# Two transformer blocks on one core: norm factor applied to the products' results, stages of block two placed beside dense chunks

## The chip, the cores and the metric

One core of a Trainium2 chip runs the whole computation. The metric is device time in microseconds, the median of three runs. The engines are TensorE (PE: matmul, and PEld: its weight load), VectorE (DVE), ScalarE (ACT), GpSimd (POOL) and SyncE (SP), whose queue issues the DMAs.

## What is computed

x has 512 tokens of width 1024, float32. Block one:

```python
z = rms_norm(h, attn_norm) @ w_in
o = concat(nsa_mixer(...), gla_mixer(...))
h = h + o @ w_out
u = causal_dwconv(rms_norm(h, ffn_norm) @ w_up, conv_w, conv_b)
h = h + (silu(gate) * up) @ w_down
```

`nsa_mixer` is softmax attention with compressed, selected and window parts; `gla_mixer` is gated linear attention in chunks of 64. Block two puts 16 meta tokens in front, so that it has 528:

```python
proj = rmsnorm(h, gain) @ w_in
q, k = l2norm(silu(conv4(dq))), l2norm(silu(conv4(dk)));  v = silu(conv4(dv))
o_dn = rmsnorm(gated_delta_rule(q, k, v, g, beta)) * silu(dz)
o_sb = stick_breaking_attention(rmsnorm(sq), rmsnorm(sk), sv)
merged = sigmoid(gate_dn) * (o_dn @ w_branch_dn) + sigmoid(gate_sb) * (o_sb @ w_branch_sb)
h = h + merged @ w_out
h = h + (silu(gate) * up) @ w_ffn_out
```

Every `rms_norm` is x * rsqrt(mean(x^2) + eps) * gain: a factor per token and a gain per channel.

## The kernel before

**Layout and the stream of weights.** Activations lie with channels on partitions: `K.h` holds the residual as 8 tiles of 128 x 512. All dense weights come as one stream of 285 chunks of 128 x 1024 floats (512 KB). SP loads chunk n into one of two raw buffers (`load_chunk`, L251 to L256); ScalarE rounds it to the fast float format (`whi`, L269); VectorE writes the remainder (`wlo`, L276). Three such pairs are in use (HL = 3): when TensorE has used chunk s (`K.s_used`), ScalarE makes chunk s + 3 (`split_hi`, `split_lo`). A product is three matmuls, w_hi x_hi, w_hi x_lo and w_lo x_hi (`three`, L291 to L293), so the input x has a high and a low part too (`K.nx_hi`, `K.nx_lo`). A chunk is 8 k-tiles of one output tile of 128 channels: 24 matmuls for 512 tokens, 48 for 528 tokens in two halves of 264.

**Stages.** Each stage is a `Block`: all engines start it together, each runs its own list in order, and semaphores tie them; at the end all meet. `sems` clears the semaphores of a past stage on GpSimd. The order of the stages:

1. `start` (L493): loads x, constants, parameters; squares of x, sums over channels with matmuls (`norm_sums`, L445), root, reciprocal, factor spread over partitions with matmuls (`norm_spread`, L454), then `norm_scale` multiplies x by gain and factor (L484), ScalarE rounds (`norm_hi`, L467), VectorE subtracts (L479). The same for the meta tokens.
2. `project1`: 16 chunks with tokens on the output partitions (`product_rows512`, L413 to L415) and 8 chunks with channels there (`product_cols`).
3. `nsa_prepare`, `nsa_compressed`, `nsa_attend`, `gla`: the mixers of block one.
4. `out_ffn` (L574): the output product (8 chunks) added to `K.h`, after each tile its square and its sums on TensorE; then `norm_spread` and `norm_scale`; the up product (44 chunks, with the 3-tap convolution read from PSUM, L720 to L742); the down product (22 chunks), again with squares and sums per tile, and at the end the norm for block two.
5. Block two, `delta_gates`: one chunk for the gates' logits, small matmuls, and a chain of activations.
6. For each of two groups of four heads: `project_conv` twice (8 chunks each, 4-tap convolution and SiLU, L1481 to L1492), `norm_cols` (squares, sums with 16-column matmuls L1397, root, reciprocal L1422, spread with 16-row matmuls L1405, scaling L1429), `delta_rows` (transposes as matmuls L1612, scaled copies), `delta_rule` with 8 chunks of the gate `dz` placed among its small matmuls (`Side`, L1697; ScalarE copies the results, L1990), `delta_output` (row norm, SiLU, transposes L2106), then the branch product: 8 chunks for group 0, and 16 chunks in `merge_pairs` for group 1 (gate and branch in turn).
7. Attention: `project_plain` three times (8 chunks each), `transpose_units`, `norm_cols` over 16 heads, `stick_breaking`, `split_stage`, `merge_last` (16 chunks: 8 gates, 8 branch).
8. `out_ffn` for block two (no convolution, no next norm), with the store of the result.

In a `product_cols` stage two pairs of PSUM banks alternate, and ScalarE (or VectorE) frees them with a copy; `out_ffn` rotates over four banks. VectorE, ScalarE and TensorE queues are strictly in program order, so a step waits for every step that stands before it on its engine.

## Time and profile before

| | us |
|---|---|
| median of 3 runs | 2732.98 (2722.13 to 2749.69) |
| the profiled execution | 2740.02 |
| its span in the trace | 2737.9 |
| mean granted TensorE clock | 0.91 |

A group's row gives line, engine, operation, output<-input, shapes and count, then busy time and the mean of one, then the idle time of the engine before it and what ended it. A window's row gives start:end and length, then for each engine busy time and instruction count, then the granted TensorE clock (1.00 is 2.4 GHz, 0.50 is 1.2 GHz), the share of DMA engines busy, and GB/s. A timeline's row gives start and duration. One float32 matmul with float32 operands leaves two records in the trace (two passes).

### The profile page before, as it was taken

To read this page: it belongs to the slowest core of one execution; us is meant where nothing else is said; L and a number is where in the kernel's file an instruction comes from. 1 tells how busy PE (TensorE), PEld (TensorE's weight loads), DVE (VectorE), ACT (ScalarE), POOL (GpSimd) and SP (SyncE) were. 2 spreads that over 40 slices of the span, in tenths; PEclk is the share of its full clock that TensorE was granted. 3 is DMA by queue.
4 is the path that set the end of the run, shared out by engine and by line. 5 is a ranking of instruction groups with operands and counts; after the bars stand their busy time and mean duration, and the time that the engine had idled before them with its cause. 6 is when DMAs were issued, how large, how long until landed. Compare 5 with 4: busy or idle time off the path is not lost. (4 is left out here: it accounts for less than half of the span.)

```text
span 2737.9 us, 32980 instructions
## 1 busy us (share of the span) xinstructions
PE 2441.1 (89%) x13996; PEld 1887.7 (69%) x13996; DVE 1042.2 (38%) x1588; ACT 829.1 (30%) x1350; POOL 36.2 (1%) x68
## 2 busy tenths in 40 slices
PE   5976997799999968799698799699989989999999
PEld 4854555578888858666478666488966467788887
DVE  3234353445553235434525444432122124433322
ACT  2223234134442233222323222322233632322221
POOL 0000000000000000000000000000001200000000
PEclk9986598599999979789899899899997999999999
DMA  3231000022333212000022011032210022223322
GB/s 118 93 93 47 1 1 1 24 70 93 98 95 93 93 39 78 23 32 25 9 85 78 24 32 32 16 92 78 85 39 0 1 77 85 69 93 96 97 93 92
DMA packets 48354, 163.31 MB, mean 60 GB/s; under 512 B 5072, under 2 KB 9552, under 8 KB 48208
## 3 DMA queue, kind: packets, MB, share of 16 engines
q1 hardware_dynamic: 48208, 161.20, 18.6%
q8 instruction: 111, 1.82, 0.3%
q14 instruction: 35, 0.29, 0.0%
HBM read 158.04 MB, written 2.10 MB: 58 GB/s over the span
## 5 line engine op out<-in xcount | busy, mean ns | idle before, releaser
L291 PE MATMUL ps<-nx_hi,whi 128*128 128x512 f32 (+1 forms) x1936 | 680.0, 351 | 74.1 <-ACTq L361 24.1
L292 PE MATMUL ps<-nx_lo,whi 128*128 128x512 f32 (+1 forms) x1936 | 676.2, 349 | 0.0
L293 PE MATMUL ps<-nx_hi,wlo 128*128 128x512 f32 (+1 forms) x1936 | 675.0, 349 | 0.0
L276 DVE TENSOR_TENSOR wlo<-raw,whi 128x1024 fp32r<-128x1024 f32 x282 | 345.1, 1224 | 781.0 <-ACT whi L269 781.0
L269 ACT ACTIVATE whi<-raw 128x1024 fp32r<-128x1024 f32 x282 | 298.1, 1057 | 764.3 <-PE ps L293 693.1
L291 PEld LDWEIGHTS ps<-nx_hi,whi 128*128 128x128 f32 x1936 | 374.1, 193 | 128.9 <-issue 67.3
L292 PEld LDWEIGHTS ps<-nx_lo,whi 128*128 128x128 f32 x1936 | 375.4, 194 | 46.0
L293 PEld LDWEIGHTS ps<-nx_hi,wlo 128*128 128x128 f32 x1936 | 374.6, 193 | 46.0
L291 PE MATMUL ps<-act_hi,whi 128*128 128x512 f32 x352 | 139.6, 396 | 0.0
L292 PE MATMUL ps<-act_lo,whi 128*128 128x512 f32 x352 | 139.1, 395 | 0.0
L293 PE MATMUL ps<-act_hi,wlo 128*128 128x512 f32 x352 | 139.0, 395 | 0.0
L291 PE MATMUL ps<-o_hi,whi 128*128 128x512 f32 x192 | 77.0, 401 | 7.8 <-ACTq L361 7.8
L293 PEld LDWEIGHTS ps<-act_hi,wlo 128*128 128x128 f32 x352 | 66.0, 187 | 16.2
L292 PEld LDWEIGHTS ps<-act_lo,whi 128*128 128x128 f32 x352 | 66.0, 188 | 15.9
L291 PEld LDWEIGHTS ps<-act_hi,whi 128*128 128x128 f32 x352 | 66.0, 188 | 15.8
L292 PE MATMUL ps<-o_lo,whi 128*128 128x512 f32 x192 | 76.8, 400 | 0.0
L293 PE MATMUL ps<-o_hi,wlo 128*128 128x512 f32 x192 | 76.6, 399 | 0.0
L1154 ACT ACTIVATE probs<-ps,max 128x128 f32<-128x128 f32 (+3 forms) x64 | 33.8, 528 | 120.9 <-DVE max L1111 120.9
L1405 PE MATMUL ps<-rt,const_sb 16*128 16x264 f32 x128 | 57.4, 646 | 14.0 <-DVE rt L1423 14.0
L1062 PE MATMUL ps<-kT,qT 64*128 64x128 f32 (+3 forms) x128 | 62.6, 575 | 1.4 <-PEq L969 1.4
L1405 PEld LDWEIGHTS ps<-rt,const_sb 16*128 16x128 f32 x128 | 42.0, 331 | 28.8 <-DVE rt L1423 15.6
L1697 PE MATMUL ps<-nx_hi,whi 128*128 128x512 f32 x128 | 58.0, 453 | 2.8 <-PEq L1596 2.8
(428 smaller groups left out, 3019.6 us busy)
## 6 DMA issues: line engine op xcount, KB each, us to landing
raw<-stream_dram SPq DMA_DIRECT2D x285, 512.0 KB, 3.5
h_sb<-x_dram SPq DMA_DIRECT2D x4, 512.0 KB, 5.4
cmp_w<-cmp_w_k_dram SPq DMA_DIRECT2D x4, 512.0 KB, 4.5
cmp_w<-cmp_w_v_dram SPq DMA_DIRECT2D x4, 512.0 KB, 3.9
out_dram<-h_sb SPq DMA_DIRECT2D x8, 256.0 KB, 4.9
const_sb<-const_dram SPq DMA_DIRECT2D x1, 816.5 KB, 8.4
param_sb<-param_dram SPq DMA_DIRECT2D x1, 774.0 KB, 9.7
const<-const_dram SPq DMA_DIRECT2D x1, 616.0 KB, 4.0
```

Source lines behind the costliest of these rows:

```text
L269: act.activation(K.whi[:, n % HL], K.raw[:, n % RAW], ACT.Copy).then_inc(K.s_hi, 1)
L276: dve.tensor_tensor(K.wlo[:, n % HL], K.raw[:, n % RAW], K.whi[:, n % HL].bitcast(F32), ALU.subtract).then_inc(K.s_lo, 1)
L291: pe.matmul(out, whi, xhi, start=start, stop=False, skip_group_check=skip)
L292: pe.matmul(out, whi, xlo, start=False, stop=False, skip_group_check=skip)
L293: return pe.matmul(out, wlo, xhi, start=False, stop=stop, skip_group_check=skip)
L1062: pe.matmul(out, R.qT[b0:b0 + 64, h // 2, t * P:(t + 1) * P], R.kT[b0:b0 + 64, 2 * b + g, 0:ext], start=True, stop=False, skip_group_check ...
L1154: act.activation(pr[:, u % 2, b, 0:(t + 1) * P], K.ps[:, 2 * (u % 2) + b, 0:(t + 1) * P], ACT.Exp, bias=mx[:, u % 2, b:b + 1], accum_out=s ...
L1405: mm = pe.matmul(K.ps[:, 2 + 2 * (i % 3) + h, 0:HALF], cst(K, "ident", 16)[:, i:i + 1].broadcast_to([16, P]), rt[:, a:e], start=True, stop ...
L1697: mm = pe.matmul(K.ps[:, 6 + c % 2, :], w, x, start=j == 0, stop=j == SIDE_CHUNK - 1, skip_group_check=True)
```

## The change

**Norm factor on the result.** Products take x times gain, without the token factor. `residual_hi` and `residual_lo` make its parts from `K.h` directly; the squares are summed over the 8 tiles on VectorE (`residual_acc`), so that `norm_sums` needs 8 matmuls in all. The factor is spread once into `K.fac` (SBUF), and VectorE multiplies each product's result by it when it leaves PSUM.

```diff
+def residual_hi(K, act, z, d, gain, ready):
+    act.wait_ge(z["added"], ready)
+    act.activation(K.nx_hi[:, d, META:T2], K.h[:, d], ACT.Identity, scale=gain[:, d:d + 1]).then_inc(z["nx_hi"], 1)
...
+    act.activation(K.sq[:, d % 2], K.h[:, d], ACT.Square).then_inc(z["squares"], 1)
+def residual_lo(K, dve, z, d, gain):
+    dve.wait_ge(z["nx_hi"], d + 1)
+    dve.scalar_tensor_tensor(K.nx_lo[:, d, META:T2], K.h[:, d], gain[:, d:d + 1], K.nx_hi[:, d, META:T2].bitcast(F32),
+                             ALU.mult, ALU.subtract).then_inc(z["nx_lo"], 1)
+def residual_acc(K, dve, z, d):
...
+    dve.tensor_tensor(K.acc[:], K.sq[:, 0] if d == 1 else K.acc[:], K.sq[:, d % 2], ALU.add).then_inc(z["acc"], 1)
```

**Start and first products are one stage**, `start_project1`. The gains load first, the first weight chunks between the tiles of x, the constants and the other parameters later; the first product waits for two tiles of `nx_lo`. The sums come behind the fourth chunk; the fifth waits for the mean squares. The row products are scaled by ScalarE as they leave PSUM (per-partition factor), the 8 column products by VectorE.

```diff
+                    pe.wait_ge(K.s_lo, s + 1)
+                    if gi == 0:
+                        pe.wait_ge(z["nx_lo"], 2 * u + 2)
+                    elif u == 4:
+                        pe.wait_ge(z["mean_square"], 1)
+                        pe.wait_ge(z["meta_mean"], 1)
```

**out_ffn.** No sums between output tiles. The up product starts as tiles of `nx_lo` come; the sums stand behind its first chunk, the spread in the middle of its second. Every up result gets an extra multiply, and the convolution reads SBUF:

```diff
+                    if u == 1 and k == KT // 2:
+                        pe.wait_ge(z["factor"], 1)
+                        norm_spread(K, pe, 5).then_inc(z["spread"], 1)
...
+                        dve.tensor_tensor(zb[:, kind], K.ps[:, j % 4, :], K.fac[:, META:T2], ALU.mult).then_inc(z["z"], 1)
+                        if kind == 0 and p:
+                            low_part(p - 1)
```

Behind block one's down product only the split of x times gain is left; the sums for block two's factor follow in the next stage, behind its first chunk.

**Block two has fewer stages.** `front(K, S, grp)` replaces `delta_gates`, two `project_conv`, `norm_cols` and `delta_rows`; for group 1 also `delta_output` and the branch product of group 0, and it holds the 8 gate chunks that `merge_pairs` had. Its chunks, in order:

```diff
+    lead = [("ab", 0)] if grp == 0 else [("gate", i) for i in range(KT)] + [("branch", i) for i in range(KT)]
+    plan = lead + [("conv", i) for i in range(16)]
...
+                if kind == "conv":
+                    dve.tensor_tensor(zc[:, i % 2, 3:].rearrange("p (a b) -> p a b", a=2), both, fac2, ALU.mult).then_inc(z["free"], 1)
+                    if i >= 1:
+                        convolve(i - 1)
+                make_lo(K, dve, first + u)
+                if kind == "gate":
+                    output.dve(dve, i)
+                if r >= 0:
+                    beside(r)
```

k comes before q in the stream now. The first tap is ScalarE's (Identity with a scale), three taps are VectorE's. Behind conv chunk r TensorE runs `beside(r)`: the gates' matmuls at r = 1 and 4 (group 0), head-norm sums at r = 5 and 9, spreads at 7, 8, 11, 12, the row units of k at 10 and 13, of the first half of v at 14, the rest behind the last chunk:

```diff
+    def sums(self, pe, b):
+        for h, (a, e) in enumerate(FULL):
+            for c in range(4):
+                mm = pe.matmul(self.K.ps[32 * c:32 * c + 32, 4 + h, 0:HALF], cst(self.K, "pick"), self.sq[:, c, a:e],
+                               start=True, stop=True)
+    def factor(self, act, b):
...
+        K.act_chain.link(act, act.activation(rt, K.ps[:, 4:6, 0:HALF], ACT.Ln, bias=self.eps))
+        act.activation(rt, rt, ACT.Exp, scale=-0.5, bias=float(np.log(self.scales[b]))).then_inc(self.z["n_factor"], 1)
+    def spread(self, pe, b, pair):
...
+            for c in (2 * pair, 2 * pair + 1):
+                mm = pe.matmul(self.K.ps[:, 4 + 2 * (c % 2) + h, 0:HALF], cst(self.K, "first_row")[32 * c:32 * c + 32],
+                               self.rt[32 * c:32 * c + 32, a:e], start=True, stop=True)
```

`DeltaOutput` is the old `delta_output` in six steps beside the first six chunks (gate chunks in `front` for group 1, q chunks in the attention stage): steps 0 and 1 squares with their sums on ScalarE, 2 and 3 scaling of rows and SiLU on ScalarE, 4 and 5 transposes on TensorE, gating and splitting.

`second_attention_products` is one stage of 32 chunks (8 q, 8 branch of group 1, 8 k, 8 v) with `DeltaOutput`, the head norms of q and k (four batches of sums, eight spreads) and the transposes of v beside them. `merge_second` holds `split_stage` and `merge_last`. In `delta_rule` VectorE multiplies the `dz` chunks' results by `K.fac`, where ScalarE copied them:

```diff
-                            act.activation(fill.dst[:, c], K.ps[:, 6 + c % 2, :], ACT.Copy).then_inc(fill.s_out, 1)
+                            dve.wait_ge(K.s_used, first + c + 1)
+                            dve.tensor_tensor(fill.dst[:, c], K.ps[:, 6 + c % 2, :], K.fac[:, META:T2], ALU.mult).then_inc(fill.s_out, 1)
```

**Memory.** The residual is written to a DRAM tensor at the start of block two and read back in `merge_second` (2 MB each way, first in SP's queue of that stage); its place in SBUF holds the gates meanwhile. Scratch tiles of the mixers lie in the space of `nx_hi`/`nx_lo` and of a new mixer buffer `K.mx`, those of block two in one arena. The code of `nsa_*`, `gla`, `stick_breaking` and the inversion in `delta_rule` is otherwise the same.

## Rows read from the trace of the kernel before

**Rows 1.** The page: busy us (share of the span) and instructions of each engine.
```profile
PE 2441.1 (89%) x13996; PEld 1887.7 (69%) x13996; DVE 1042.2 (38%) x1588; ACT 829.1 (30%) x1350; POOL 36.2 (1%) x68
```
**Rows 2.** Windows, one per stage: start:end, length, engines' busy (count), clock, DMA, GB/s.
```profile
0.00:47.80 47.80, 17.08 (x90) 16.52 (x91) 17.93 (x30) 14.00 (x21) 0.20 (x4) 1.00 0.30 112
47.80:188.40 140.60, 137.27 (x576) 110.15 (x576) 28.18 (x23) 34.86 (x34) 0.00 (x0) 0.99 0.29 95
188.40:532.80 344.40, 270.90 (x1250) 169.42 (x1250) 158.06 (x378) 98.36 (x283) 0.00 (x0) 0.72 0.06 16
532.80:989.60 456.80, 437.59 (x1921) 354.46 (x1921) 213.02 (x258) 157.98 (x198) 0.00 (x0) 0.97 0.28 86
989.60:1171.30 181.70, 148.07 (x1129) 135.76 (x1129) 83.48 (x124) 59.29 (x88) 0.00 (x0) 0.83 0.16 50
1171.30:1339.00 167.70, 160.46 (x1718) 102.21 (x1718) 64.49 (x146) 37.53 (x81) 5.12 (x4) 0.94 0.08 26
1339.00:1580.00 241.00, 190.72 (x1260) 168.97 (x1260) 112.70 (x142) 79.30 (x107) 0.00 (x0) 0.84 0.16 53
...
1742.00:2082.90 340.90, 295.56 (x1736) 256.94 (x1736) 101.25 (x108) 91.80 (x116) 0.00 (x0) 0.89 0.20 62
...
2198.00:2301.40 103.40, 91.25 (x384) 73.10 (x384) 40.38 (x48) 31.89 (x42) 0.00 (x0) 0.96 0.26 82
2301.40:2737.90 436.50, 428.53 (x1848) 344.82 (x1848) 136.97 (x149) 109.33 (x134) 0.00 (x0) 0.98 0.29 91
```
**Rows 3.** Windows of parts: up and down product, attention one, hand-over, delta output.
```profile
592.90:841.60 248.70, 247.97 (x1057) 199.17 (x1058) 148.33 (x184) 106.57 (x136) 0.00 (x0) 0.99 0.30 90
2611.50:2734.80 123.30, 123.28 (x529) 98.68 (x527) 30.36 (x29) 21.70 (x21) 0.00 (x0) 1.00 0.29 93
267.00:337.00 70.00, 68.24 (x187) 38.25 (x188) 20.70 (x63) 14.66 (x46) 0.00 (x0) 0.50 0.00 1
337.00:456.00 119.00, 118.09 (x615) 71.41 (x613) 59.93 (x166) 39.79 (x118) 0.00 (x0) 1.00 0.00 1
...
970.30:989.60 19.30, 4.73 (x24) 4.30 (x24) 12.51 (x20) 8.21 (x12) 0.00 (x0) 0.55 0.00 0
1339.00:1370.10 31.10, 7.02 (x32) 5.58 (x32) 22.31 (x29) 17.27 (x19) 0.00 (x0) 0.58 0.00 1
```
**Rows 4.** Timeline of ScalarE at the start: start us, us, what, idle before.
```profile
4.83 0.63 ACT L520 ACTIVATE sq<-h_sb 128x512 f32<-128x512 f32 x1 [2.81 <-DMA h_sb<-x_dram]
...
9.00 0.63 ACT L520 ACTIVATE sq<-h_sb 128x512 f32<-128x512 f32 x1 [0.68 <-DMA h_sb<-x_dram]
```
**Rows 5.** Timeline of ScalarE in a convolution stage.
```profile
1102.14 0.59 ACT L1481 ACTIVATE z<-ps 128x528 f32<-128x528 f32 x1
...
1107.03 1.06 ACT L269 ACTIVATE whi<-raw 128x1024 fp32r<-128x1024 f32 x1
1107.99 0.59 ACT L1481 ACTIVATE z<-ps 128x528 f32<-128x528 f32 x1
```
**Rows 6.** Groups by line, window 1069 to 1171 (convolution, head norms, rows).
```profile
L1405 PE MATMUL ps<-rt,const_sb 16*128 16x264 f32 x32 | 14.4, 647 | 4.7 <-DVE rt L1423 4.7
L1491 DVE SCALAR_TENSOR_TENSOR y<-z,param_sb,y 128x528 f32<-128x528 f32 x16 | 12.3, 769 | 0.6
...
L1397 PE MATMUL ps<-sq,const_sb 128*16 128x264 f32 x32 | 10.2, 495 | 8.1 <-ACT sq L1415 8.1
L276 DVE TENSOR_TENSOR wlo<-raw,whi 128x1024 fp32r<-128x1024 f32 x8 | 9.8, 1226 | 23.5 <-ACT whi L269 23.5
...
L1612 PE MATMUL ps<-const_sb,v_cols 128*64 128x128 f32 x128 | 7.2, 272 | 0.0
```
**Rows 7.** Groups of TensorE, window 2301 to 2361.5 (block two's output product).
```profile
L445 PE MATMUL ps<-const_sb,sq 128*128 128x1 f32 x64 | 7.7, 241 | 0.9 <-ACT sq L677 0.9
```
**Rows 8.** Timeline of ScalarE in the gates' stage of block two.
```profile
1004.24 1.28 ACT L1575 ACT_TABLE_LOAD   x1
1005.53 0.24 ACT L1575 ACTIVATE e<-e 128x40 f32<-128x40 f32 x1
```

More of the change, by code:

```diff
@@ L244, in link @@
         eng.wait_ge(self.sem, self.count)
-def over_chunks(eng, first, n, step):
-    for c in range(n):
-        step(c, first + c, 0)
 def load_chunk(K, sp, n):
@@ L293, in three, with chunk_product @@
     return pe.matmul(out, wlo, xhi, start=False, stop=stop, skip_group_check=skip)
+def chunk_product(K, pe, s, bank, x_hi, x_lo, ranges):
+    pe.wait_ge(K.s_lo, s + 1)
+    for i, (a, e) in enumerate(ranges):
+        for k in range(KT):
+            mm = three(pe, K.ps[:, bank + i, 0:e - a], K.whi[:, s % HL, k * P:(k + 1) * P], K.wlo[:, s % HL, k * P:(k + 1) * P],
+                       x_hi[:, k, a:e], x_lo[:, k, a:e], k == 0, k == KT - 1)
+    mm.then_inc(K.s_used, 1)
 def sems(K, *names):
@@ L438 @@
-NORM_SEMS = ("squares", "sums", "mean_square", "root", "factor", "spread", "normed", "nx_hi", "nx_lo")
-SUM_BANK, SPREAD_BANK = 4, 5
-def norm_sums(K, pe, z, d, sq):
-    for t in range(TT):
-        mm = pe.matmul(K.ps[:, SUM_BANK, t:t + 1], sq[:, t * P:(t + 1) * P], cst(K, "ones")[:, 0:1],
-                       start=d == 0 and t == 0, stop=d == KT - 1, skip_group_check=True)
-    mm.then_inc(z["sums"], 1)
-def norm_spread(K, pe, z):
-    pe.wait_ge(z["factor"], 1)
-    for t in range(TT):
-        mm = pe.matmul(K.ps[:, SPREAD_BANK, t * P:(t + 1) * P], K.t_rs[:, t:t + 1].broadcast_to([P, P]), cst(K, "ident"),
+FULL = [(0, HALF), (HALF, T2)]
@@ new lines, in start_project1 @@
+def start_project1(K, R, v):
+    first, n_rows, n_cols = K.at, 16, 8
+    z = named_sems(K, "gains_in", "consts_in", "params_in", "const1_in", "meta_in", "added", "x_in_1", "x_in_2", "x_in_3",
+                   "nx_hi", "nx_lo", "squares", "acc", "sums", "mean_square", "root", "factor", "spread", "fac",
+                   "rows_free", "cols_free", "meta_squares", "meta_sums", "meta_mean", "meta_root", "meta_factor",
+                   "meta_spread", "meta_scaled", "meta_normed", "meta_hi")
+    z["x_in_0"] = K.live[5]
+    g0, gn = PARAM_COLS["g_attn"][0], 4 * KT
@@ L574, in out_ffn @@
-def out_ffn(K, x_hi, x_lo, conv, gain_ffn, gain_next, out):
+                dve.memset(K.fac[:, 0:META], 1.0)
+                dve.wait_ge(z["gains_in"], 16)
+                for k in range(KT):
+                    residual_lo(K, dve, z, k, gain)
+                    if k in (1, 3):
+                        dve.wait_ge(K.s_hi, k // 2 + 1)
+                        dve.tensor_tensor(K.wlo[:, k // 2], K.raw[:, k // 2], K.whi[:, k // 2].bitcast(F32), ALU.subtract).then_inc(K.s_lo, 1)
+                    if 1 <= k < KT - 1:
+                        residual_acc(K, dve, z, k)
@@ L644, in _ @@
                     mm.then_inc(K.s_used, 1)
+                    if u == 0:
+                        pe.wait_ge(z["acc"], KT - 2)
+                        pe.wait_ge(z["squares"], KT)
+                        norm_sums(K, pe, 4).then_inc(z["sums"], 1)
                 for d in range(KT):
@@ new lines, in _ @@
+            for u, (kind, i) in enumerate(plan):
+                s, bank, r = first + u, 2 * (u % 2), u - n0
+                if u >= 2:
+                    pe.wait_ge(z["free"], u - 1)
+                if kind == "branch":
+                    if i == 0:
+                        pe.wait_ge(z["o_hi"], KT)
+                        pe.wait_ge(z["o_lo"], KT)
+                    chunk_product(K, pe, s, bank, K.mx_hi, K.mx_lo, [(0, SEQ)])
+                else:
+                    chunk_product(K, pe, s, bank, K.nx_hi, K.nx_lo, TOKENS if kind == "gate" else FULL)
+                if grp == 0 and u == 0:
+                    norm_sums(K, pe, 4).then_inc(z["sums"], 1)
+                if kind == "gate":
+                    output.pe(pe, i)
+                if r >= 0:
+                    beside(r)
```

1551 lines of the change are left out of this document (855 added, 696 removed), and 5 rows, old and new, of the table ROW_UNITS.

## The prediction

> **What bounds the kernel now.** I read the page's totals first [rows 1]: TensorE is busy 89% of 2737.9 us, nobody else reaches 40%. So TensorE's stream is the bound, and only two things can be won: its idle 297 us (2737.9 less 2441.1) and the time in which its granted clock is 0.5 (1.2 GHz) while it works. Then I cut the span into the kernel's stages [rows 2] and asked of each how far its length stands above its dense chunks at full clock. Two prices per chunk of weights are needed. A chunk of 512 tokens: 22 chunks of the down product take 123.3 us with TensorE never idle and clock 1.00 [rows 3], 5.60 us each. A chunk of 528 tokens (two halves of 264): ScalarE copies one chunk's result at 1102.14 and the next at 1107.99 [rows 5], 5.85 us. The row-major products of the start stage have 24 chunks in 140.6 us with one gap and a short cold stretch [rows 2], some 136 us of chunks.
>
> The stages between dense products stand out [rows 2, 3]: 47.8 us before the first product; 19.3 us after block one's down product with clock 0.55; 31.1 us of delta output with 7.0 us of TensorE; a stage of 340.9 us that holds 40 chunks, about 226 us of them. The mixers of block one (344.4 us), the two delta rules and the stick-breaking stage aren't restructured.
>
> **The change, part by part.** Sums are against the profiled execution, 2740.0 us; the median of the runs is 2733.0, 7.0 lower, which I take off at the end.
>
> *Start and first products, 188.4 us.* Now no token factor is needed before the products: x times gain is split, and the factor is applied to the result. x arrives at 4.83 us [rows 4]; two nx_hi, one square and one whi on ScalarE (0.63 each, 1.06 for a whi [rows 4, 5]) and a last 1.23 us wlo on VectorE [rows 6] put the first product at about 9.5 us. The first weight chunk now travels between the x tiles, which 9.00 for the fourth tile pair against 4.83 for the first [rows 4] shows to be 1.4 us per 0.5 MB. Chunks 136; before the fifth chunk TensorE waits for both mean squares behind one whi/wlo pair and a table load, 4.7, and 1.7 for the clock behind that wait; spreading the factor 1.5. Sum 153.4: 35.0 saved. The later constants and parameters queue on SP between chunks and are wanted only in the next stage.
>
> *Block one's output, FFN and hand-over, 456.8 us.* Out goes the norm on TensorE's path. It was one set of sums per output tile, 64 records 7.7 us for eight tiles [rows 7], plus a chain factor, spread, eight scalings. After: 8 chunks 44.8, cold start 3.0 (the clock is already low there), the up product 248.7 [rows 3] less 2.0 that it lost to a cold first chunk, sums of 16 records at 0.12 [rows 7] 1.9, spread 1.5, down 123.3, and down to the next product 4.3 (residual add, scaled copy, subtract, change of block) where 19.3 stood. 425.5: 31.3 saved. VectorE pays: it is busy 148.3 of 248.7 us [rows 3], 3.4 us per chunk, and gets a 0.71 us multiply for each: 4.1 of 5.65. It is hidden by TensorE; without that cover 44 chunks would cost 31 us.
>
> *Block two, first front, 181.7 us.* Seventeen chunks of 5.85, 99.5; cold 2.9; sums, spread and the wait for the factor copy 1.9 + 1.5 + 1.6; the gates' small matmuls 2.8 (their chain of five table loads leaves the path); head norms, two batches of sums and four spreads; rows that now lie between chunks, 136 records at 0.056 [rows 6], 7.7; a tail. The head norms are priced nowhere in this form: 32 output columns, or 32 rows, where the trace has 16 of either. A batch of sums is 16 passes; one after another at 0.32 [rows 6] that is 5.1 us, and if four column groups run at once 1.3. The 64-column transposes give 0.056 us per pass of 128 [rows 6], so halves of the array do run together; I take 1.3, being nearest to that row, and 1.3 for a spread too (bounds 0.9 and 3.6 from 0.45 per pass at half clock [rows 6]). Six of them 7.8. The tail is serial: result times factor 0.71, two convolutions of three taps at 0.77 [rows 6] with a wlo between, 6.7 in all, SiLU 0.8, the last rows 3.9, their copy 0.7, block change 1.9: 14.0. Sum 139.7: 42.0 saved.
>
> The Trainium skill's page "TensorE: Matmul & The Clock Gate", section "Why this matters for your kernels", says that matmuls whose outputs lie in different groups of 32 partitions run at once. By it a batch of sums is 1.3 us; if the trace is read serially it is 5.1 and the eight batches of the change cost 30 us more. The 64-column rows agree with it; no row shows 32.
>
> *Second front with delta output beside, 241.0 us.* It now holds 32 chunks instead of 24: 89.6 + 93.6, block change 2.8, cold 1.7, output transposes 4.0, head norms 7.8, rows 7.7, tail 14.0: 221.2, 19.8 saved. The 31.1 us of delta output [rows 3] lie beside eight gate chunks. ScalarE there has 27 us of steps (16 squares, 16 scalings, SiLU in two parts, three table loads) in four chunks' 22.4, and its next whi waits behind them in order; the weights are three chunks ahead, so this costs nothing. If that lead were gone it would be 5 us.
>
> *Second output, attention products, 340.9 us.* 32 chunks: 24 x 5.85 + 8 x 5.60 = 185.2; 2.8 + 1.7; output 4.0; four batches and eight spreads 15.6; value rows inline 2.2, tail 6.5. 218.0: 122.9 saved, eight chunks of it moved to the stage before. The norms' 62 us after the third product and two block changes are what goes.
>
> *Merge and second FFN.* 103.4 becomes 3.0 + 1.7 + 89.6 + 5.4 = 99.7 (3.7 saved): the reload of h, 2 MB at 1.4 us per half MB, goes first in SP's queue and holds the weights back 5.6 us, inside the three chunks' lead of 17; likewise the store in the first front. The last 436.5 become 44.8 + 2.5 + 246.7 + 3.4 + 123.3 + 3.1 = 423.8: 12.7.
>
> *Delta rules, 167.7 us* (and 162.0 for the second, the same pattern). The gate-chunk copy moves from ScalarE to VectorE, which is in the inversion chain. Eight times 0.71 is 5.7 at worst, 0 at best (a copy that falls in a wait), perhaps less than nothing since ScalarE is freed; I take 2.0 each, -4.0.
>
> Sum: 35.0 + 31.3 + 42.0 + 19.8 + 122.9 + 3.7 + 12.7 - 4.0 = 263. Against it, in three blocks some fifteen semaphores meet queues that work in order; I allow 5 us for each block, as each has one or two places where the margin is below 2 us (the tail, row copies behind a 7 us VectorE round in a 5.85 us chunk, the second half of the output transposes). 248 net: 2740 - 248 - 7 = **2485 us**; its own range 2455 to 2520.
>
> **Rivals.**
> *Evacuation and ScalarE steps run late in the merged blocks.* For: VectorE has 4.3 us of work per conv chunk (0.71, three taps of 0.77, wlo 1.23), ScalarE 3.0 plus, per head-norm batch, Ln and Exp. In the trace a change of function reloads a table at 1.28 us; of five such loads in a row one stands with what follows it [rows 8]. Against: four PSUM banks and three chunks of lead. If handshakes make a conv chunk 7.0, 32 x 1.15 = 37, and 10 for the gate chunks: 2532.
>
> "ScalarE: Activation LUTs", section "What ACT_TABLE_LOAD costs" of the Trainium skill, gives a switch 2.66 us with its drain, and its section "Table sets: the hidden batching unit" says that Ln followed by Exp loads once. The trace disagrees on both (the load at 1004.24 stands between an Exp and the Ln behind it, and that Ln starts 0.01 us after it ends [rows 8]), and the measurement decides.
>
> *TensorE's clock in block one's attention.* That code is untouched, yet it ran 70 us at 0.50 with 187 matmuls and then 119 us at 1.00 with 615 [rows 3], without a change in the work; what ended the low stretch isn't in the rows, and the stage now begins 35 us earlier. If it stays low to the end it costs up to 119; half of that is 2545. If it starts high, 35 less: 2450. Against a big shift: the three runs lie within 28 us.
> *The work beside chunks isn't hidden.* It is TensorE's own queue, in order, so each late signal stops the dense stream just as a stage did. Then only start, FFN and last norms are won, 35 + 31 + 13 = 79: 2654.
> *Slower.* The multiply that frees a bank makes VectorE the bound in every scaled dense chunk, about 144 (88 up, 32 conv, 24 attention). The point from which it decides is 250/144 = 1.7 us beyond TensorE's pace, 7.4 us per chunk; at 8.0 it is 2485 + 144 x 2.2 = 2802. Against: 4.1 us of VectorE per up chunk now.
>
> **How the numbers follow.** Forecast 0.58, late queues 0.18, clock 0.15 (0.10 up, 0.05 down), not hidden 0.06, slower 0.03. The range takes in late queues, most of the clock case and the bounds on head norms (30 us): 2445 to 2570. A measurement of this kernel tells about 1% from no change; all cases but the last lie beyond that: faster 0.96, within 1% 0.01, slower 0.03.
>
> **What would show it.** Right: first product near 10 us; products done near 153; up product still 5.6 us per chunk with TensorE always busy; no idle stretch of TensorE above 3 us in the three merged blocks but at their tails; head-norm sums under 2 us a batch; VectorE's share up to about 45%. Wrong: conv chunks above 6.5 us, TensorE waiting on VectorE's multiply, or a first-attention stage away from 344 us by over 20.

## The result, and the profile after

The changed kernel takes 2456.9 us (median of four executions, 2430.1 to 2477.7); the kernel before it took 2741.3 on the same chip (2722.1 to 2751.2). The ratio is 0.894, with a 95% interval of 0.883 to 0.904. The profiled execution of the changed kernel is its slowest, 2477.7 us with a span of 2475.9; the windows below are of it. Its four executions have mean granted clocks of 0.935, 0.939, 0.948 and 0.956 and times of 2477.7, 2466.1, 2447.6 and 2430.1 us: the time follows the clock.

The page's totals of the changed kernel, which answer to [rows 1]:

```profile
PE 2333.4 (94%) x13804; PEld 1806.5 (73%) x13804; DVE 1105.7 (45%) x1713; ACT 865.3 (35%) x1446; POOL 36.2 (1%) x68
```

TensorE's idle time fell from 297 to 142.5 us (2475.9 less 2333.4). The other 107.7 us went from its busy time, through 192 instructions less and much less time at the low clock (495 us of it before, 322 now). VectorE has 63.5 us more, as it should: the multiplies by the factor.

Windows of the changed kernel, one per stage (start:end, length, busy of each engine with its count, granted clock, DMA share, GB/s). They answer to [rows 2]:

```profile
0.00:38.50 38.50, 27.05 (x129) 22.17 (x129) 17.95 (x25) 19.37 (x29) 0.20 (x4) 1.00 0.61 226
38.50:153.00 114.50, 114.47 (x490) 92.23 (x490) 29.47 (x31) 29.61 (x37) 0.00 (x0) 0.99 0.28 88
153.00:529.60 376.60, 303.98 (x1249) 187.05 (x1250) 158.95 (x379) 98.34 (x282) 0.00 (x0) 0.65 0.05 14
529.60:948.80 419.20, 414.03 (x1800) 336.01 (x1800) 240.51 (x298) 158.29 (x198) 0.00 (x0) 1.00 0.29 93
948.80:1089.70 140.90, 131.12 (x1153) 125.17 (x1153) 80.64 (x122) 74.77 (x112) 0.00 (x0) 0.94 0.24 79
1089.70:1250.70 161.00, 154.21 (x1718) 99.72 (x1718) 67.94 (x152) 34.09 (x73) 5.12 (x4) 0.98 0.09 28
1250.70:1473.40 222.70, 210.59 (x1453) 186.85 (x1453) 120.28 (x154) 109.36 (x176) 0.00 (x0) 0.98 0.23 76
1473.40:1636.60 163.20, 157.36 (x1718) 101.31 (x1718) 67.84 (x152) 34.02 (x73) 5.11 (x4) 0.96 0.08 27
1636.60:1851.50 214.90, 209.81 (x1546) 192.39 (x1545) 93.83 (x115) 85.85 (x133) 0.00 (x0) 0.99 0.25 79
1851.50:1963.70 112.20, 106.41 (x368) 54.13 (x368) 21.15 (x40) 76.84 (x168) 25.73 (x56) 1.00 0.00 1
1963.70:2058.70 95.00, 90.31 (x385) 73.25 (x384) 45.13 (x56) 31.92 (x36) 0.00 (x0) 0.98 0.33 111
2058.70:2475.90 417.20, 414.03 (x1800) 336.22 (x1800) 162.03 (x192) 112.84 (x134) 0.00 (x0) 1.00 0.29 95
```

| stage | before | forecast | after |
|---|---|---|---|
| start and first products | 188.4 | 153.4 | 153.0 |
| block one's mixers | 344.4 | 344.4 | **376.6** |
| out, FFN, hand-over | 456.8 | 425.5 | 419.2 |
| first front | 181.7 | 139.7 | 140.9 |
| first delta rule | 167.7 | 169.7 | 161.0 |
| second front | 241.0 | 221.2 | 222.7 |
| second delta rule | 162.0 | 164.0 | 163.2 |
| second attention's products | 340.9 | 218.0 | 214.9 |
| stick-breaking | 115.1 | 115.1 | 112.2 |
| merge | 103.4 | 99.7 | 95.0 |
| last out and FFN | 436.5 | 423.8 | 417.2 |

One row is off by 32 us, and it is a stage whose code didn't change. Windows of parts of the changed kernel, as [rows 3]. The first begins 10.5 us into the up product, which runs from 574.5 to 821.8, and ends 10.8 us into the down product; then come the down product, two parts of the first attention, and the hand-over:

```profile
585.00:832.60 247.60, 247.60 (x1073) 200.91 (x1073) 175.64 (x222) 107.22 (x134) 0.00 (x0) 1.00 0.29 94
821.80:943.60 121.80, 121.80 (x529) 99.00 (x527) 42.03 (x46) 33.50 (x39) 0.00 (x0) 1.00 0.29 95
...
229.80:384.30 154.50, 152.41 (x428) 86.39 (x428) 46.31 (x133) 31.74 (x96) 0.00 (x0) 0.50 0.00 1
384.30:457.00 72.70, 71.05 (x373) 43.07 (x372) 35.69 (x97) 23.79 (x70) 0.00 (x0) 1.00 0.00 1
943.60:948.80 5.20, 0.04 (x1) 0.00 (x0) 3.75 (x5) 2.30 (x4) 0.00 (x0) 0.88 0.00 0
```

Read the two attention rows as rates: 428 matmul records in 154.5 us at 0.50, then 373 in 72.7 us at 1.00. TensorE counts as busy 98% of both. Before, the clock rose after 70 us of this stage [rows 3]; here after 154.

TensorE's longest waits in the changed kernel (what it waited for, us in total, times, longest):

```profile
PE ps L893 <- DVEq L827: 15.1, 1, 15.1
PE ps L1553 <- issue: 14.5, 2, 7.2
PE ps L1226 <- DVE rows L1292: 14.2, 1, 14.2
PE ps L443 <- DVE wlo L514: 10.6, 1, 10.6
...
PE ps L278 <- PEq L1954: 6.3, 2, 3.2
...
PE ps L278 <- PEq L575: 5.2, 1, 5.2
```

L893 and L1226 are in block one's mixers, which weren't touched. L1553 is the tail of each front, L443 the first product, L1954 the change of block behind a delta rule, L575 the hand-over. Between the first chunk and the tail no merged block has a wait in this list; the longest that its trace shows there is 1.5 us in the first front, 0.7 in the second and 0.8 in the second attention's products.

### The profile page after: what moved, and what is told of

Read it like the earlier page. It is cut to its first block and busy times, and to the rows that moved or that the text cites. A ratio compares the mean times of both kernels' runs of the same rounds, so it can differ in the third digit from the quotient of the medians.

```text
span 2475.9 us, 32735 instructions
## 1 busy us (share of the span) xinstructions
PE 2333.4 (94%) x13804; PEld 1806.5 (73%) x13804; DVE 1105.7 (45%) x1713; ACT 865.3 (35%) x1446; POOL 36.2 (1%) x68
## 3 DMA queue, kind: packets, MB, share of 16 engines
q1 hardware_dynamic: 48640, 165.46, 20.5%
## 5 line engine op out<-in xcount | busy, mean ns | idle before, releaser
L278 PE MATMUL ps<-nx_hi,whi 128*128 128x512 f32 (+1 forms) x1808 | 618.1, 342 | 14.0 <-PEq L1954 6.3
L279 PE MATMUL ps<-nx_lo,whi 128*128 128x512 f32 (+1 forms) x1808 | 615.9, 341 | 0.0
L280 PE MATMUL ps<-nx_hi,wlo 128*128 128x512 f32 (+1 forms) x1808 | 614.7, 340 | 0.0
L278 PE MATMUL ps<-mixer_out,whi 128*128 128x512 f32 x384 | 152.2, 396 | 5.5 <-PEq L2528 3.8
L280 PE MATMUL ps<-mixer_out,wlo 128*128 128x512 f32 x384 | 151.7, 395 | 0.0
L279 PE MATMUL ps<-mixer_out,whi 128*128 128x512 f32 x384 | 151.6, 395 | 0.0
L703 DVE TENSOR_TENSOR z<-ps,fac 128x512 f32<-128x512 f32 x88 | 60.9, 692 | 166.6 <-PE ps L280 166.5
L278 PEld LDWEIGHTS ps<-mixer_out,whi 128*128 128x128 f32 x384 | 72.0, 188 | 24.7 <-issue 6.1
L280 PEld LDWEIGHTS ps<-mixer_out,wlo 128*128 128x128 f32 x384 | 72.1, 188 | 17.5
L279 PEld LDWEIGHTS ps<-mixer_out,whi 128*128 128x128 f32 x384 | 72.1, 188 | 17.2
L2005 PEld LDWEIGHTS ps<-mixer_floats 64*64 64x64 f32 x1664 | 54.2, 134 | 27.7 <-ACT mixer_floats L2207 13.4
L1056 PE MATMUL ps<-mixer_floats,rows 128*64 128x128 f32 x320 | 66.6, 357 | 0.0
```

The costliest lines, as they stand in the source:

```text
L278: pe.matmul(out, whi, xhi, start=start, stop=False, skip_group_check=skip)
L279: pe.matmul(out, whi, xlo, start=False, stop=False, skip_group_check=skip)
L280: return pe.matmul(out, wlo, xhi, start=False, stop=stop, skip_group_check=skip)
L703: dve.tensor_tensor(zb[:, kind], K.ps[:, j % 4, :], K.fac[:, META:T2], ALU.mult).then_inc(z["z"], 1)
L1056: mm = pe.matmul(out, vv, pt[:, u % 2, b, kt * P:(kt + 1) * P], start=b == 0 and kt == 0, stop=b == 1 and kt == t, skip_group_check=True)
L2005: mm = pe.matmul(quads(b)[half[p], q], lhs[half[p], q], rhs[half[p], q], start=True, stop=True)
```

## The experiments

The runs below are compared by a stage table like the one above (TensorE's first matmul of each stage) and by the low-clock time that falls into a stage. In such a table the first attention runs from its first scores to the first product of the gated linear attention: 189.1 us before, 226.2 after.

**Control.** The changed kernel unaltered, twice, beside the experiments.

> The changed kernel itself, unaltered, as the control that the runs beside it are read against. Both theories: 2430 to 2478 us, as its four executions so far. The clock theory adds that the profiled time follows the low-clock time of the trace: about 322 us of low clock at 2476 us of span, and the attention stretch (230 to 457 us) anywhere between 192 us, as before the change, and 227 us, as in the first profile after it, by how long the clock stays low there.

Measured: 2464.4 us (2431.6 to 2475.7) and, on another occasion with five rounds, 2460.2 (2432.9 to 2477.2). All stages but one agree with the first profile within 3.5 us. The attention took 210.8 us with 119 us at the low clock in one profile, and 226.3 with 154 in the other. So the stage differs from one execution to the next of the same program, within the expected bounds. It isn't the only one that does. The first of the two profiles has an attention 15.5 us shorter and yet a span only 2 us shorter (2473.9 against 2475.9): its other stages are 13 us longer together, and its low-clock time is 327 us in all, against 322. The gated linear attention is 3.4 us longer there, with 15 us more at the low clock, and the two output products take 47.6 and 47.4 us with 6 us at the low clock each, where the first profile has 44.9 twice and none.

**A dense piece ahead of the attention.**

```diff
                 for u in range(2):
                     for b in range(2):
                         scores(u, b)
+                for _ in range(16):
+                    pe.matmul(K.ps[:, 7, :], K.whi[:, 0, 0:P], K.whi[:, 1, 0:SEQ], start=True, stop=True, skip_group_check=True)
```

> Sixteen extra matmuls of 512 columns (about 3.5 us of work at full clock, twice that at half) into an unused bank, ahead of the transposes of the first block's attention; nothing is left out. Theory A (the 32 us that block one's mixers took more than in the profile before are only TensorE's clock, which stays low from 210 to 384 us because TensorE works in short pieces there): a dense piece ahead of the attention raises the clock, the stretch 230 to 384 us falls towards its length at full clock, and the whole by 30 to 77 us to about 2400 us. Rival B (the clock falls back by itself once the attention's short pieces begin, whatever stood ahead): the low stretch starts again within some 10 us, and the whole is longer by the fill, 3 to 7 us.

Measured: 2420.0 us (2418.9 to 2428.9) where the control of the same chip took 2464.4. The window of the attention with the fill:

```profile
230.60:396.50 165.90, 164.21 (x816) 99.94 (x816) 80.76 (x228) 54.26 (x164) 0.00 (x0) 0.97 0.00 1
```

and of the control's two profiles:

```profile
230.90:441.70 210.80, 208.02 (x800) 121.33 (x800) 81.23 (x228) 54.64 (x164) 0.00 (x0) 0.72 0.00 1
```

```profile
230.10:456.40 226.30, 223.51 (x800) 129.53 (x801) 81.34 (x228) 55.00 (x164) 0.00 (x0) 0.66 0.00 1
```

Sixteen matmuls more, VectorE's and ScalarE's work the same within 1.5%, and the stage is 45 and 60 us shorter. The clock was low when the fill began at 236.97 us, rose at 241.1 while it ran (5.83 us of fill), and stayed up to the stage's end. Theory A is confirmed, the rival is out: the attention's own pieces keep a high clock up, but don't reliably raise a low one.

**The same piece in the kernel before.**

> The kernel before the change, with the same sixteen extra matmuls ahead of its attention; nothing is left out. Theory A (the clock in the attention is a matter of the attention alone): the 92 us of low clock in its attention go, the stage gets about 46 us shorter less 4 to 6 of fill, and the whole is about 2700 us; the attention then has the same length as in the changed kernel with the fill, 166 us. Rival B (the low stretch belongs to what the change did to the stages around it): under 10 us here.

Measured: 2710.3 us (2707.1 to 2714.4) against 2744.2, ratio 0.988 (0.983 to 0.994). The attention of the kernel before with the fill:

```profile
264.40:429.70 165.30, 163.62 (x816) 99.53 (x816) 80.80 (x228) 54.33 (x164) 0.00 (x0) 0.97 0.00 1
```

165.3 against 165.9 in the changed kernel: the same stage in both once the clock is up. Theory A holds, though my sizes were off: of the 92 us at the low clock only 69.6 lay in the attention (267.7 to 337.3), so it fell by 23.8 us, not by 46. Now the change can be read without the attention's chance: 2710.3 to 2420.0, 290 us, where the plain medians give 284. The two figures are from two sets of runs on one chip. By the medians the fill gave the kernel before 33.8 us and the changed kernel 44.4; whether the stage is on average longer at the low clock after the change isn't shown, as the kernel before has one unfilled profile.

All unfilled profiles together put a size on it: (low-clock us in the attention, its length) is (34, 173.5) in the run of the keys' norm below, (44, 177.6) in that of the delta output, (69.6, 189.1) in the kernel before, (105, 204.6) in the run of the factor, (119, 210.8) in the control and three more, and (154, 226.3). That is a line of 0.44 us per low-clock us.

**The delta output ahead of the chunks.** Its steps leave the chunk loops of both stages and run in one piece before them:

```diff
+            if grp:
+                output.pe(pe, 4)
+                output.pe(pe, 5)
+                pe.wait_ge(z["o_hi"], KT)
+                pe.wait_ge(z["o_lo"], KT)
             for u, (kind, i) in enumerate(plan):
...
-                if kind == "gate":
-                    output.pe(pe, i)
```

> The delta output of each group done in one piece ahead of the first chunk of what follows, in place of one step behind each chunk; nothing is left out. Theory A (the placement beside chunks is what removed the openings): both places get back what the profile before showed as the opening of the second front and of the attention products, 24 us each, so the whole is longer by some 40 to 55 us than the changed kernel on the same chip, and the trace shows TensorE idle for about 20 us at 1251 and at 1637 us. Rival B (the openings went because the first weights and the chunks' buffers are ready earlier, so the place of the output is worth nothing): longer by under 5 us.

Measured: 2522.3 us (2483.9 to 2533.9) against the control's 2464.4 (2431.6 to 2475.7); with so wide a spread, the attention's draw in it, the medians give no price. Read by stages, delta rule and what follows it counted together, it is 410.9 against 386.3 us and 406.0 against 381.2 in the first control profile, so 24.6 and 24.8 more, as theory A said. Against the other two profiles of the changed kernel (383.6 and 378.1, with less low clock in these stages) it is 27.3 and 27.9. TensorE's waits at the first of the two places:

```profile
PE ps L1465 <- ACT arena L1415: 21.2, 1, 21.2
PE ps L278 <- ACT mixer_out L1423: 5.4, 1, 5.4
PE ps L1465 <- DVE arena L1448: 1.9, 1, 1.9
```

The first is for ScalarE's scaled rows; with 6.5 us of TensorE's transposes in between, the opening is 35.1 us (1200.6 to 1235.7) at a clock of 0.61, where the changed kernel has one of 3.1. The chunks behind it then run 4 to 6 us shorter; they no longer carry the transposes. The placement of the delta output is worth 49 to 55 us of the two stages.

**The factor ahead of the up product.**

```diff
+                pe.wait_ge(z["nx_lo"], KT)
+                pe.wait_ge(z["acc"], KT - 2)
+                pe.wait_ge(z["squares"], KT)
+                norm_sums(K, pe, 4).then_inc(z["sums"], 1)
+                pe.wait_ge(z["factor"], 1)
+                norm_spread(K, pe, 5).then_inc(z["spread"], 1)
+                pe.wait_ge(z["fac"], 1)
                 for u in range(2 * FT):
...
-                        if u == 0:
-                            pe.wait_ge(z["nx_lo"], k + 1)
```

The up product thus no longer starts on the first tiles of `nx_lo` either, and ScalarE's root and VectorE's factor stand ahead of the split of the first up weights.

> In both feed-forwards the norm's factor is waited for ahead of the first up product, where the changed kernel takes the sums behind the first chunk and spreads the factor in the second; nothing is left out, and the factor is still multiplied onto the results. Theory A (of the 15 us saved at each hand-over only the smaller part is the delay of the factor, the larger part is that the norm is 8 sums and no scaling of the eight tiles): longer by 5 to 10 us for each feed-forward, 10 to 20 us together. Rival B (the delay of the factor is the whole of it): 14 us or more for each, 28 us or more together.

Measured: 2478.4 us (2476.3 to 2484.7), 14.0 above the control. From the output product's first chunk to the up product's it is 55.7 and 56.9 us, where the control has 47.6 and 47.4; the up product is 0.9 shorter. So 7.1 and 8.6 for the two feed-forwards. TensorE's waits in the first of them:

```profile
PE ps L340 <- DVE nx_lo L381: 3.8, 1, 3.8
...
PE ps L278 <- DVE fac L367: 0.8, 1, 0.8
PE ps L348 <- DVE t_rs L362: 0.7, 1, 0.7
```

These 5.3 us and the sums and the spread themselves are the price. Most of the waiting is for the last `nx_lo` tile, not for the factor. The size is theory A's. From the output product's start to the up product's it was 60.1 us before (532.8 to 592.9 [rows 2, 3]) and is 44.9 in the profile after; of these 15.2 us the deferred factor and the start on the first tiles give 7 to 9. That is about half, where theory A called it the smaller part. Some 4 us are the clock (estimated as half of 8.9 us at the low level before, none after). Only what is left, 2 to 4 us, can come from 8 matmuls of sums in place of 32 and from dropping the eight scalings; no run tries that part by itself.

**More load on VectorE.**

```diff
+                        for _ in range(1 if p < 8 else 2 if p < 15 else 3):
+                            K.dve_chain.link(dve, dve.tensor_tensor(K.acc[:], K.ps[:, j % 4, :], K.fac[:, META:T2], ALU.mult))
                         dve.tensor_tensor(zb[:, kind], K.ps[:, j % 4, :], K.fac[:, META:T2], ALU.mult).then_inc(z["z"], 1)
```

> Extra copies of the multiply by the factor on VectorE, into a scratch tile, ahead of each up chunk's own multiply in both feed-forwards: one for the first 16 chunks, two for the next 14, three for the last 14. Nothing is left out. VectorE has 4.0 us of work per up chunk in the changed kernel, TensorE 5.6. Theory A (the multiply is hidden until VectorE's own time passes TensorE's): with one extra 4.8 us and with two 5.6 us per chunk TensorE loses under 0.3 us per chunk; with three VectorE is the bound at 6.5 us or more per chunk. Rival B (the multiply frees the PSUM bank, so any delay of it reaches TensorE): 0.7 us per chunk for each extra one, from the first on.

Measured, in one execution of 2491.3 us, in windows of 16, 14 and 14 chunks of the first FFN, and of the last 14 of the second:

```profile
563.90:653.60 89.70, 89.70 (x401) 73.21 (x401) 71.40 (x96) 39.16 (x49) 0.00 (x0) 1.00 0.27 92
653.60:733.00 79.40, 79.40 (x345) 64.36 (x344) 68.97 (x92) 31.62 (x40) 0.00 (x0) 1.00 0.27 86
733.00:826.60 93.60, 82.11 (x340) 62.23 (x338) 82.81 (x112) 33.77 (x43) 0.00 (x0) 1.00 0.25 79
2285.00:2364.00 79.00, 79.00 (x343) 64.05 (x342) 63.23 (x84) 23.78 (x28) 0.00 (x0) 1.00 0.29 94
```

5.61, 5.67 and 6.69 us per chunk: one extra costs nothing, two cost under 0.1, three cost 1.1. In the second FFN, which has no convolution (VectorE 4.5 us per chunk with three extras), three cost nothing either: its up product is 247.3 us as ever. So the multiply itself holds nothing up; what decides is VectorE's list against TensorE's 5.6. VectorE is busy 4.9 us per chunk with two extras and 5.9 with three, so the turning point lies between. Its own busy time isn't the whole of the list: with three extras it waits another 0.6 us per chunk for ScalarE's part of the convolution, and the two together are 6.5 of the 6.69. What TensorE then waits for isn't a PSUM bank but the low part of the next weights, which stands behind the multiplies in VectorE's queue:

```profile
PE ps L278 <- DVE wlo L273: 10.0, 12, 1.3
```

VectorE's own waits in the stretch with three extras:

```profile
DVE up L710 <- ACT up L655: 6.2, 7, 0.9
DVE gate L710 <- ACT gate L646: 2.0, 7, 0.3
```

**The keys' head norm behind the last chunk.** Sums, factors, spreads and scalings of k leave the value chunks and stand behind them, all ten turned value units follow:

```diff
-                if u in (21, 26):
...
             pe.wait_ge(z["free"], len(plan))
-            v_rows_of(4, 10)
+            pe.wait_ge(z["q_n_normed"], 8)
+            for b in range(2):
+                norms[1].sums(pe, b)
+                norms[1].spread(pe, b, 0)
+                norms[1].spread(pe, b, 1)
+            pe.wait_ge(z["k_n_normed"], 8)
+            v_rows_of(0, 10)
```

> In the second attention's products the norm of the keys' heads is done as a stage behind the last chunk, with all the turned value rows behind it, where the changed kernel has it beside the value chunks; nothing is left out. Theory A (hidden work becomes a chain of squares, sums, Ln, Exp, spread and scaling, in two batches): the stage becomes longer by 20 to 32 us, and TensorE does about 6 us of work in that time. Rival B (the norm costs nearly the same beside the chunks, since TensorE's stream is held up by it there too): under 10 us longer.

Measured in its trace: 232.4 us from the stage's first chunk to the stick-breaking's first product, against 211.7, so 20.7 more, at the lower end of theory A. TensorE's waits there:

```profile
PE ps L1512 <- ACT h_sb L1504: 5.4, 2, 2.7
PE ps L1493 <- ACT h_sb L1485: 3.4, 1, 3.4
PE ps L1512 <- DVE arena L1526: 3.3, 2, 1.6
...
PE ps L1493 <- DVE arena L1526: 1.6, 1, 1.6
PE ps L2412 <- DVE arena L1526: 1.5, 1, 1.5
```

15.2 us of waits, and 31 us at the low clock in the stage, where the unaltered kernel has 3 to 6. The whole took 2447.3 us in the profiled execution (attention 173.5 us) and 2496.5 to 2497.8 in three others: by the median alone, against a control of another set of runs, the price would read as 33.

**Order of the head-norm sums.**

```diff
-        for h, (a, e) in enumerate(FULL):
-            for c in range(4):
+        for c in range(4):
+            for h, (a, e) in enumerate(FULL):
```

> The eight matmuls of each batch of head-norm sums in another order: the two halves of one group of 32 output partitions behind each other, where the changed kernel goes through all four groups and then again; nothing is left out and each result is the same. Read from the trace, batch by batch. Theory A (matmuls for different groups of output partitions run at once, so that a batch takes the time of two of them, and only neighbours in the queue can): with pairs for one group next to each other a batch takes about twice the 1.1 us of the changed kernel, 2.0 to 2.6 us. Rival B (the order doesn't matter, the array takes any that is ready): 1.1 us still. In the whole either is below what one execution tells.

Measured, in one execution of 2475.5 us: each of the eight batches spans 1.12 to 1.13 us, 1.10 in the changed kernel (from the start of the first to the end of the last of its 16 matmul records). Theory A has fallen as far as it says that only neighbours in the queue run at once: both orders take the same time. The group of L1493 in the first front of this run, and then, in the changed kernel's first front, those of L1512 (the spreads) and L1493:

```profile
L1493 PE MATMUL ps<-arena,const_sb 128*32 128x264 f32 x32 | 2.2, 393 | 0.0
```

```profile
L1512 PE MATMUL ps<-mixer_floats,const_sb 32*128 32x264 f32 x32 | 4.6, 407 | 0.0
...
L1493 PE MATMUL ps<-arena,const_sb 128*32 128x264 f32 x32 | 2.2, 392 | 0.0
```

32 records of 0.39 us take 2.2 us of busy time, so between five and six records overlap at any time. The Trainium skill's page "TensorE: Matmul & The Clock Gate", section "Why this matters for your kernels", has matmuls of distinct groups of output partitions run at once; the trace agrees (1.1 us a batch, where one after another at 0.32 [rows 6] would be 5.1).

**The residual read back four times.**

```diff
-            sp.dma_start(K.h[:], K.h_dram).then_inc(z["h_in"], 16)
+            for n in range(4):
+                if n:
+                    sp.wait_ge(z["h_in"], 16 * n)
+                sp.dma_start(K.h[:], K.h_dram).then_inc(z["h_in"], 16)
...
```

> The residual is read back from DRAM four times, one after another, ahead of the weights in SP's queue, at the start of the last merge, where the changed kernel reads it once; nothing is left out. One read takes 7.9 us to landing, so the weights' loads start some 31 us later in the block than they otherwise do, against three chunks of weights already loaded, 16 to 17 us. Theory A (a read ahead of the weights is hidden up to the three chunks' lead and costs what goes beyond it): the merge is 10 to 16 us longer, with one wait of TensorE for a weight chunk near the fourth chunk, and one read alone costs nothing. Rival B (no lead is left at that place): 24 us or more. Rival C (the weights come in fast enough for the queue to be caught up): under 3 us.

Measured, in one execution of 2485.4 us: the merge is 113.6 us against 94.1, 19.5 more: between theories A and B. The windows up to TensorE's stop, and its stop:

```profile
1950.10:1968.60 18.50, 18.48 (x72) 14.61 (x72) 0.69 (x1) 1.15 (x2) 0.00 (x0) 0.91 0.72 258
1968.60:1985.10 16.50, 0.03 (x2) 0.02 (x1) 1.30 (x2) 2.39 (x4) 0.00 (x0) 0.56 0.71 283
```

Three chunks (72 records) are done in 18.5 us, then one wait of 16.5. The mechanism is A's; I had left out the fourth chunk's own transfer and its two splits by ScalarE and VectorE, and the clock behind the wait. It also gives the margin of the single read. The fourth chunk's low part was ready 35.0 us after the block began, with weights issued 23.2 us later than in the changed kernel; there it is thus ready at about 12 (in its trace, at 1976.2, 11.6 us after the block's first instruction on SP), and TensorE asks for it at about 18. Some 6 us of lead are left, and one read costs nothing: the changed kernel's merge has no wait of TensorE for weights.

**More fills.** Eight matmuls ahead of the compressed scores, and sixteen in each of two waits of the gated linear attention:

```diff
                 mm.then_inc(s_o2, 1)
+                pe.wait_ge(s_ev, 8)
+                for _ in range(8):
+                    pe.matmul(K.ps[:, 7, :], K.whi[:, 0, 0:P], K.whi[:, 1, 0:SEQ], start=True, stop=True, skip_group_check=True)
...
                 mm.then_inc(s_x, 1)
+                for _ in range(16):
...
                 mm.then_inc(s_b, 1)
+                for _ in range(16):
```

> The changed kernel with the sixteen extra matmuls ahead of the attention, and three more pieces of such extra matmuls in waits of TensorE: eight ahead of the compressed scores (at about 208 us), sixteen behind the gates' product and sixteen behind the cumulative sums of the gated linear attention. Nothing is left out. Theory A (a short stage whose clock is low is long by half of TensorE's own time in it): against the version with the first fill alone the compressed scores, 19 us of TensorE at the low level, get 8 us shorter, the gated linear attention up to 10 us, the whole 8 to 18 us, about 2405 us. Rival B (the clock falls again in the waits that follow, and the fills only delay what is behind them): same as with the first fill alone, or up to 10 us longer.

Measured: 2416.7 us (2415.2 to 2417.8), 3.3 below the version with one fill (in another set of runs); the gated linear attention went from 73.2 to 71.7, the stage ahead of the attention from 74.9 to 74.3. Theory A had asked for 8 to 18 us, so the rival is nearer: the clock rose at 222.8 and was down again at 226.2. TensorE's longest waits in those stages, 15.1 and 14.2 us for VectorE, are as long as without the fills; that they set the stages' length is argued from that, not tried.

> The changed kernel unaltered, as the control beside the version with fills on the same chip: 2430 to 2478 us, spread by the clock in the attention.

> The version with all four fills again, beside the changed kernel on the same chip. Theory A (the fills take the chance out of the clock in the attention): 2415 to 2418 us with a spread under 5 us, 1.5 to 2% below the changed kernel's median. Rival B (the earlier gain was one chip's): within 0.5% of the changed kernel.

Measured, both on one chip: the version with fills 2417.9 us (2416.0 to 2419.1), the changed kernel 2460.2 (2432.9 to 2477.2). It beats both kernels: ratio to the kernel before 0.882 (0.879 to 0.886), and it is 1.7% below the changed kernel's median and 15 us below its fastest execution.

## Why the prediction was right, and where it was off

The forecast was 2485 us and the range 2445 to 2570; the median is 2456.9. The case forecast is the one that came, at the very edge of its own range of 2455 to 2520, and one of the prediction's own signs of being wrong came with it: the first attention's stage, 376.6 us, is away from 344 by more than 20. The other signs are those of being right: first product at 10.6, products done at 153.0, up product 5.6 us per chunk with TensorE always busy, sums 1.1 us a batch, VectorE's share 45%.

*Start.* The first product begins at 10.56 us (forecast about 9.5), the stage ends at 153.0 (153.4). Between the fourth and the fifth chunk lie 3.2 us, most of it the sums themselves and 0.9 of it a wait for the mean squares, where 4.7 were put for the wait. The 1.7 for the clock behind it fits: 3.4 us ran at the low level.

*Feed-forwards.* The terms of the first add up to 425.5 and it took 419.2; the second 423.8 and 417.2. Of the first 6.3 us, 2.9 are the cold start of the output product (3.0, and 2.5 in the second), which this profile doesn't have: the eight chunks took 44.9, no more than their full-clock time, in both. That is a draw too and not a wrong size: in the first control profile they took 47.6 and 47.4, 2.8 and 2.6 more, as forecast. The up product with sums and spread took 247.3, 2.8 less than summed, the down product 121.8, 1.5 less. The hand-over took 5.2 (4.3). VectorE's 4.0 us per chunk (4.1) are hidden, as the VectorE run shows: it costs something only between two and three extras. The prediction's 1.7 us beyond TensorE's pace is another point, at which the whole gain would be gone; three extras, at 1.1 us beyond TensorE's pace, don't get there.

*Fronts.* 140.9 and 222.7 for 139.7 and 221.2. The head-norm price that the trace of before didn't show was right in kind: 1.1 a batch (1.3), 4.6 for four spreads, 1.15 each (1.3). The first tail, 7.2 of wait, 7.1 of rows and a change of block, is 15.3 for 14.0, and the second, with less of it at the low clock, 14.1.

*Second attention's products.* 214.9 for 218.0: the norms' 62 us and the block changes are gone. The key-norm and the delta-output runs, which undo the placement of one piece each, are 20.7 and 24.8 us longer at this place, so the placement earns this much of the 122.9 at least; the rest of it (eight chunks gone to the stage before, the queries' norm, two changes of block) no run undoes.

*Delta rules.* I took +2.0 each for the copy that moved to VectorE. Measured: -6.7 and +1.2. The low-clock time in them went from 20.5 to 7 us and from 7 to 14; half of these differences is -6.8 and +3.4, so by this estimate the copy itself cost between 0 and -2, as if it fell into a wait; no run tries it.

*Merge.* 95.0 for 99.7: around the chunks' 89.6 the opening took 0.9 us, not 3.0, and the end 3.8, not 5.4. The reload is hidden, with 6 us to spare, though one read takes 7.9 us to landing where 5.6 were summed.

*Block one's attention* failed as a term: I carried 344.4 over unchanged, and the profile after has 376.6. The rival named it, with the reason left open, and gave it 0.15. The runs show what it is: a stage that starts at the low clock and leaves it after 34 to 154 us, differently from execution to execution, at 0.44 us per low-clock us. Both kernels have it. I had read one profiled execution as the stage's length; 189.1 us before was one draw.

*The other rivals.* Late queues would have made 32 chunks with their side work 37 us longer; the second front and the attention's products came within 1.5 and 3.1 us of their sums. "Not hidden" and "slower" would have shown as waits of TensorE on VectorE's multiply, and there are none until VectorE is given three more per chunk, when the wait is for its split of the weights.

*The allowance* of 15 us for late semaphores has no counterpart: none of the merged blocks has a wait above 1.5 us between its opening and its tail. Some 31 us by which the other rows came out shorter (34 less 3 longer) and 32 more in the attention's stage make the profiled 2475.9 us against a sum of 2474.9 without the allowance (2737.9 less 263): right to 1 us only because two errors cancel. That the median lies within the ranges owes something to the draw as well: of the four executions two, 2430.1 and 2447.6 us, lie below the forecast's own range, and one below 2445. With the attention's clock taken out by the fills, the change is worth 290 us where 248 were forecast.

What stays open: what ends a low stretch within the attention in one execution after 34 us and in another after 154 wasn't tried. Nor does a run undo the merging of the start with the first products (35 us) or that of the first front (41); for these the account rests on the stage table and on the waits that are gone.

## What to carry to other kernels

Work of other engines is worth placing beside dense chunks only while the fullest of them stays below TensorE's time per chunk: sum VectorE per chunk, include the weights' own split, since that is what TensorE waited for here, and add what VectorE itself waits for in that list. A DMA put ahead of the weights costs nothing up to the lead that the loaded chunks give, less the transfer and the split of the next one. Before the length of a stage of short matmuls is carried over into a forecast, look at its clock: here a short dense piece ahead of such a stage made it 24 to 60 us shorter, and the time of the whole kernel repeatable. One profiled execution is one draw: take several before a stage's length is called a fact.

## What was not expected of the hardware

The clock stayed at 1.2 GHz for 154 us while TensorE counted as busy 98% of the time, its longest wait 1.1 us. The Trainium skill's page "TensorE: Matmul & The Clock Gate", section "Why this matters for your kernels", advises to leave no idle gaps between bursts of matmuls if the clock is not to drop. The trace agrees for the stage that is at the high level: with the fill its longest wait is 1.0 us, and it runs at 0.97. But the absence of gaps doesn't tell the two states apart, since the same stage with waits no longer than 1.1 us also ran at 0.50 for 154 us, and the measurement decides. And the whole kernel's spread on one chip, 2433 to 2477 us, shrinks to 2416 to 2419 with 5.8 us of otherwise useless matmuls there and some short ones elsewhere; with the first fill alone, in another set of runs, it was 2419 to 2429.
